# Spreading the filler products of a chunked delta-rule stage one by one, with the chunks written out

## Chip, cores and metric

One NeuronCore of one Trainium2 chip. The metric is the device time of the whole kernel in microseconds (us), the median over executions on the chip. Lower is better.

## The reference, cut to what matters

One decoder block over 2048 tokens of width 1024: a mixer (four gated delta-rule heads beside a gated short convolution, one input and one output projection), a cross-attention into 256 memory tokens, and a SwiGLU feed-forward part. The change lies in the mixer:

```
A = where(strict, einsum(k_beta, k) * decay, 0)
T = triangular_solve(eye + A, eye)          # per chunk and head
u, w = T @ (v * beta), T @ (k_beta * exp(gc))
def step(state, ...):                        # one chunk after the other
    v_new = u_n - w_n @ state
    o     = qd_n @ state + a_n @ v_new
    state = state * exp(gl_n) + kd_n^T @ v_new
...
y = sc_b * causal_depthwise_conv(sc_c * sc_h, conv_sc_w)   # short convolution
```

The chip kernel works in tiles of 128 tokens, which it also calls chunks. The precision is that of fp32: a wide product is three TensorE passes over a high and a low half of each operand.

## The kernel before

The tokens are done in two halves of 1024. In each half come the projection of q, k, v and z, then **the chunk stage** (8 chunks of 128 tokens, four heads at once), then the output projection, attention and the feed-forward part. Every engine runs its own hand-ordered program, and semaphores tie them together.

**The steps of a chunk** are named in `STEPS`: `gram` (transposes of k and the products k·k and q·k, PE lines 1842 and 1845, and transposes of v, line 1858), `a1t` (transposes of the first level's masked matrix, line 1865), then the inverse of the triangular matrix by six doubling levels `y1 x1 ... y6 x6`. In `y` PE multiplies the odd columns of X by a masked block of A (line 1875) and transposes the even columns (line 1887). ScalarE (ACT) copies both results to SBUF (Ym line 1014, Tm line 1018). In `x` PE multiplies Tm and Ym (line 1897), and VectorE (DVE) subtracts the result from X (line 1522) and copies the next even columns (Xe, line 1429). Then come `w` (k times the state, line 1908), `v` (X times the right-hand side, line 1917) and `o` (output and state update, lines 1924, 1928, 1933). DVE makes the right-hand side for `v` in line 1532. GpSimd (POOL) makes the masked blocks `am` for the levels (line 716), the low halves of squares and weights (lines 682 and 2352), and masks the decays (lines 691 to 697).

**The fillers.** The short steps wait for each other, so PE does the short convolution's projections between them: per pair of chunks three weight units (slots 0, 1, 2), two column halves and eight k tiles, each k tile being one *slice* of three 128x512 products (lines 3018, 3019, 3020). `FILL` says how many slices follow each step. A chunk has 24 slices, which are 72 products. A filler waits for its weights' low half (`w_lo_ready`) and, where a unit begins, for the copy or product of its bank on ACT or DVE.

**The order around them.** A pair of chunks (`par` 1, then `par` 0 of the next pair) is the body of a hardware loop of three rounds. Chunk 0 and chunk 7 stand outside it. PE sums the short convolution's squares in line 1825, the norms' squares in lines 1808 and 1810, and transposes the outputs of the chunk before in line 1817.

Of the kernel before, what the change touches and what calls it, by code (L numbers as in the profile page):

```python
# [10 lines left out]
P = 128  # L11
# [161 lines left out]
CHUNK_SLICES = 3 * NCH * KT // 2  # L173
assert sum(FILL) == sum(FILL_FIRST) == CHUNK_SLICES

def block_kernel(nc, x, mem, w_units, w_ab, conv_w, sc_w, a_log, dt_bias, gdn_g, sc_g,
                 g_mix, g_mem, g_x, g_ffn, g_fin, out):
    ctx = ExitStack()
    with ctx:  # L180
# [519 lines left out]
        def chunk_pool(pool, half, m, par, j, last, split_lo):  # L700
# [20 lines left out]
            for step in STEPS:  # L721
                if step == "gram":
                    blocks(1)
                    blocks(2)
                if step in ("y1", "y2", "y3", "y4"):
                    blocks(int(step[1]) + 2)
                if step == "y4":
                    if not last:
                        squares_lo(pool, n + 1, sq_hi)
                    split_lo((n_u + 2, 2, 2) if par == 0 else (n_u + 4, 1, 1), 4)  # L730
                if step == "y6" and par == 0:
                    split_lo((n_u + 3, 0, 0), 4)
                if step == "x6" and not last:
                    decays_pool(pool, n + 1, m + 1, 1 - par)
# [202 lines left out]
        def ln_norms(act, n, b=6):  # L937
# [42 lines left out]
        def start_act(act, half):  # L980
            n = half * TT
            ln_norms(act, n, 5)
# [5 lines left out]
        def chunk_act(act, half, m, par, j, first, last, split_hi):  # L988
# [3 lines left out]
            R = half * 4 + j  # L992
            for step in STEPS:
# [15 lines left out]
                if step[0] == "y":  # L1009
                    act.wait_ge(S["y_full"], n * 6 + l)  # L1010
                    act.wait_ge(S["xy_full"], n * 6 + l - 1)
# [6 lines left out]
                    act.activation(hflat(Tm[:, :, :]), bank(2 if l == 1 else 5)[:, 0:2 * P],  # L1018
# [3 lines left out]
                if par == 0 and step == "y2":  # L1022

                    act.wait_ge(S["sc_full0"], R * 3 + 1)
                    act.wait_ge(S["sc_halo_out"], R)
                    act.activation(sc_u[:, 2:2 + CH], bank(0), ACT.Copy).then_inc(S["c_out"], 1)
                if par == 0 and step == "y6":
                    act.wait_ge(S["sc_full1"], R * 3 + 1)
                    act.activation(sc_u[:, 2 + CH:2 + 2 * CH], bank(1), ACT.Copy)\
                        .then_inc(S["c_out"], 1)  # L1030
                if par == 0 and step == "y6":
                    split_hi(nth_load(half, L_MIX + j + 1, 0), 0, 0)
                if par == 0 and not first:
# [4 lines left out]
                    if step == "y4":  # L1038
                        sc_rms(act, R - 1, 1)
# [9 lines left out]
                if step == ("y4" if first else "x3"):  # L1049
# [6 lines left out]
                if step == "y4":  # L1056
                    if not first:
                        store_o(act, half, m - 1)
                    if not last:
                        load_z(act, half, m + 1, 1 - par)  # L1060
                if step == "y5" and not last:
# [332 lines left out]
        def output_scale(dve, n):  # L1394

            k = n * 4
# [4 lines left out]
            dve.tensor_tensor(ost["v"][:, :], ost["u"][:, :], ost["t"][:, :], ALU.mult)\  # L1401
                .then_inc(S["ostep"], 1)
            dve.wait_ge(S["ostep"], k + 2)
            dve.tensor_scalar(ost["w"][:, :], ost["v"][:, :], -0.5, 1.5, ALU.mult, ALU.add)\
                .then_inc(S["ostep"], 1)
            dve.wait_ge(S["ostep"], k + 3)
            dve.tensor_tensor(ost["r"][:, :], ost["w"][:, :], ost["y"][:, :], ALU.mult)\
                .then_inc(S["ostep"], 1)

        def outputs_scaled(dve, n):  # L1410

            dve.wait_ge(S["ostep"], n * 4 + 4)
# [12 lines left out]
        def even_columns(dve, n, l):  # L1425

            dve.wait_ge(S["x_ready"], n * LEVELS + l)
            dve.wait_ge(S["xt_full"], n * 6 + l - 1)
# [50 lines left out]
        def chunk_dve(dve, half, m, par, j, first, last):  # L1479
# [7 lines left out]
            for step in STEPS:  # L1487
                l = int(step[1]) if step[0] in "yx" else 0
                if step == "gram":

                    if not first:
                        output_scale(dve, n - 1)
                    dve.wait_ge(S["gram_full"], n + 1)
                    dve.wait_ge(S["decm_ready"], n * 3 + 3)
                    dve.tensor_tensor(two(am0[:, :, :]), gram[:, :, :, 0, :], two(am0[:, :, :]),
                                      ALU.mult).then_inc(S["am0_ready"], 1)
                    dve.tensor_tensor(two(A[:, 0, :, :]), gram[:, :, :, 0, :], two(A[:, 0, :, :]),
                                      ALU.mult).then_inc(S["a_ready"], 1)
                if step == "a1t":
# [8 lines left out]
                    even_columns(dve, n, 1)  # L1508
                    if not first:
                        outputs_scaled(dve, n - 1)  # L1510
                    if par == 1:
                        sc_u_product(dve, R, 0)
                    elif not first:
                        sc_y_product(dve, R - 1, 1)
                if step == "y1":
                    dve.tensor_tensor(two(A[:, 1, :, :]), gram[:, :, :, 1, :], two(A[:, 1, :, :]),
                                      ALU.mult).then_inc(S["attn_ready"], 1)
                if step[0] == "x":

                    dve.wait_ge(S["xy_full"], n * 6 + l)  # L1520
                    dve.wait_ge(S["x_ready"], n * LEVELS + l)
                    dve.tensor_tensor(
                        odd_blocks(Xm[:, :, :], l), odd_blocks(Xm[:, :, :], l),
                        bank(4)[:, 0:NH * P // 2].rearrange("p (m c) -> p m c", c=1 << l),
                        ALU.subtract).then_inc(S["x_ready"], 1)
                    if l < LEVELS - 1:
                        even_columns(dve, n, l + 1)
                if step == "x6":
# [7 lines left out]
                    last_rest.then_inc(S["vrest_ready"], 1)  # L1536
                if step == "x1":
# [266 lines left out]
        def sums_norm(pe, n, hi=sq_hi, b=6):  # L1804
# [23 lines left out]
        def chunk_step_pe(pe, half, m, par, j, step, first, last):  # L1828
# [6 lines left out]
            if step == "gram":  # L1835

                pe.wait_ge(S["kqn_ready"], n * 2 + 2)
                pe.wait_ge(S["vrest_ready"], n)
                if first:
                    pe.wait_ge(S["egb_ready"], n + 1)  # L1840
                for hh in range(NH):
# [8 lines left out]
                pe.wait_ge(S["s_ready"], n * 4)  # L1850
                if first:
# [8 lines left out]
            if step == "a1t":  # L1860
                pe.wait_ge(S["am0_ready"], n + 1)

                pe.wait_ge(S["scln_ready"], R * 2 if par == 1 or first else R * 2 - 1)
# [3 lines left out]
            if step[0] == "y":  # L1867
                pe.wait_ge(S["x_ready"], n * LEVELS + l)
                pe.wait_ge(S["am_ready"], n * 6 + l)
                if l == 1:  # L1870
                    pe.wait_ge(S["vb_ready"], n + 1)
                else:
                    pe.wait_ge(S["ym_ready"], n * 12 + 2 * (l - 1))
# [6 lines left out]

                pe.wait_ge(S["xe_ready"], n * 6 + l)
                if l == 2:
                    pe.wait_ge(S["attn_ready"], n + 1)
                elif l > 2:
                    pe.wait_ge(S["t_ready"], n * 6 + l - 1)
                for q in range(2):
                    t = nc.tensor.transpose(bank(2 if l == 1 else 5)[:, q * P:(q + 1) * P],
                                            Xe[:, q, :], ident[:, :])
                t.then_inc(S["xt_full"], 1)
            if step[0] == "x":  # L1890

                pe.wait_ge(S["ym_ready"], n * 12 + 2 * l)
                pe.wait_ge(S["t_ready"], n * 6 + l)
                if l == 1:
                    pe.wait_ge(S["on_ready"], n)
# [4 lines left out]
            if step == "w":  # L1900

                pe.wait_ge(S["s_ready"], n * 4)
                if last:
                    pe.wait_ge(S["oo_ready"], n)
                else:
                    pe.wait_ge(S["rln_ready"], n + 2)
# [33 lines left out]
            if step == "x5" and not last:  # L1940
                if first:
                    pe.wait_ge(S["kdec_ready"], n + 1)
                else:
                    pe.wait_ge(S["oo_ready"], n)
                sums_norm(pe, n + 1)
            if step == "y3" and par == 0 and not first:
                sc_sums(pe, R - 1, 1)
            if step == "o" and par == 1 and not last:
                sc_sums(pe, R, 0)
# [320 lines left out]
        def _(pool):  # L2270
# [75 lines left out]
            def split_lo(n, pieces=1):  # L2346
# [3 lines left out]
                for i in range(pieces):  # L2350
# [3 lines left out]
                last.then_inc(S["w_lo_ready"], 1)  # L2354
# [15 lines left out]
            for half in range(NHALF):  # L2370
# [7 lines left out]
                chunk_pool(pool, half, 0, 0, 0, False, split_lo)  # L2378
                with pool.Fori(0, 3) as j:
                    chunk_pool(pool, half, j * 2 + 1, 1, j, False, split_lo)  # L2380
                    chunk_pool(pool, half, j * 2 + 2, 0, j + 1, False, split_lo)
                chunk_pool(pool, half, TT - 1, 1, 3, True, split_lo)
# [59 lines left out]
        def _(act):  # L2442
# [191 lines left out]
            for half in range(NHALF):  # L2634
# [57 lines left out]
                chunk_act(act, half, 0, 0, 0, True, False, split_hi)  # L2692
                with act.Fori(0, 3) as j:
                    chunk_act(act, half, j * 2 + 1, 1, j, False, False, split_hi)
                    chunk_act(act, half, j * 2 + 2, 0, j + 1, False, False, split_hi)
                chunk_act(act, half, TT - 1, 1, 3, False, True, split_hi)
# [80 lines left out]
        def _(dve):  # L2777
# [96 lines left out]
            for half in range(NHALF):  # L2874
# [18 lines left out]
                chunk_dve(dve, half, 0, 0, 0, True, False)  # L2893
                with dve.Fori(0, 3) as j:
                    chunk_dve(dve, half, j * 2 + 1, 1, j, False, False)
                    chunk_dve(dve, half, j * 2 + 2, 0, j + 1, False, False)
                chunk_dve(dve, half, TT - 1, 1, 3, False, True)
# [117 lines left out]
        def _(pe):  # L3015
# [291 lines left out]
            for half in range(NHALF):  # L3307
# [27 lines left out]
                def qkvz_pe(j, final):  # L3335
                    R = half * NH + j
                    for u in range(4):
                        n = unit(half, U_QKVZ + j * 4 + u)
                        pe.wait_ge(S["w_lo_ready"], n + 1)
                        for c in range(NCH):  # L3340
# [11 lines left out]
                            for k in range(KT):  # L3352
                                if final and g == 7 and k == KT // 2:
                                    gc_broadcast()
                                if final and g == 7 and k == KT - 1:
                                    sums_norm(pe, half * TT, sq_first, 5)
# [12 lines left out]
                def chunk_pe(m, par, j, first, last):  # L3369
# [3 lines left out]
                    done = par * CHUNK_SLICES  # L3373
                    for step, fill in zip(STEPS, FILL_FIRST if first else FILL_LAST if last else FILL):
                        chunk_step_pe(pe, half, m, par, j, step, first, last)
                        for s in range(done, done + fill):
                            u, c, k = s // (NCH * KT), s // KT % NCH, s % KT
# [143 lines left out]
```

## Time and profile before

| | us |
|---|---|
| median of 3 runs (2923.04 to 2924.25) | 2923.35 |
| span of the profiled execution, first to last instruction | 2921.6 |
| PE busy, of the span | 2881.8 (99%) |
| chunk stage of the first half, 316.65 to 588.49 | 271.84 |
| chunk stage of the second half, 1713.93 to 1986.10 | 272.17 |

The profiled execution's own time was not recorded apart from its span. The median of the runs is 1.75 us above the span, for what lies around the first and the last instruction. How to read the profile: PE is TensorE's matmuls and PEld its weight loads, which overlap them. The ends of matmuls are modelled and overlap the next start, so distances are read from start to start. An instruction that stands next to its predecessor has no idle note, and where there is one it is in brackets with its releaser. "issue" is idle time in which the engine waited for nothing that the profile shows.

### The profile page before, as it was taken

Reading aid. Unit: us, or ns where it says so; the run is one execution under the profiler, and the core shown is the slowest. Engines: PE = TensorE matmul, PEld = TensorE weight load, DVE = VectorE, ACT = ScalarE, POOL = GpSimd, SP = SyncE. Lnnn points to the kernel's source line nnn. Section 1 sums busy time; section 2 is a strip of 40 time slices with the busy share of each in tenths; the row PEclk is TensorE's granted clock in tenths of the full one; section 3 lists DMA queues with packets and bytes.
Section 4 is the critical chain, followed back from the end, with each engine's and each line's share of the span. In section 5 each row is a group of like instructions: output and inputs, shape, how many; then the busy total and the mean of one; then the engine's idle time right before and its main releaser. Section 6 shows DMA issues by size and latency. Waiting matters only on the chain.

```text
span 2921.6 us, 43014 instructions
## 1 busy us (share of the span) xinstructions
PE 2881.8 (99%) x14070; PEld 2394.2 (82%) x14070; DVE 1859.1 (64%) x2636; ACT 1145.3 (39%) x2049; POOL 1479.3 (51%) x1214
## 2 busy tenths in 40 slices
PE   8999999999999999999999999999999999999998
PEld 8888788888888888887888878888888888888786
DVE  2565566655359777777877556665634866665778
ACT  5532545434234333334543254443423433333334
POOL 7422455452226555568972244445322655555886
PEclk9999999999999999999999999999999999999999
DMA  7522222151113444467643232224111222224764
GB/s 260 209 96 102 94 80 72 61 177 51 58 72 114 165 152 163 165 222 246 228 144 144 100 109 73 72 65 166 65 44 74 82 108 108 97 93 146 260 192 169
DMA packets 179210, 372.41 MB, mean 127 GB/s; under 512 B 17104, under 2 KB 58128, under 8 KB 179088
## 3 DMA queue, kind: packets, MB, share of 16 engines
q1 hardware_dynamic: 116592, 301.06, 29.6%
q10 hardware_dynamic: 62496, 69.78, 7.0%
q8 instruction: 70, 1.15, 0.2%
q14 instruction: 52, 0.43, 0.0%
HBM read 268.51 MB, written 102.27 MB: 127 GB/s over the span
## 4 chain that ended last, share of the span: by engine, by line
PE 93%; DVE 2%; DMA 1%; POOL 1%; issue 1%; ACT 1%; SPq 0%; DVEq 0%; ACTq 0%; POOLq 0%
PE PS L3018 21%; PE PS L3020 21%; PE PS L3019 21%; PE PS L1991 2%; PE PS L1995 2%; PE PS L1993 2%; PE PS L1964 2%; PE PS L1962 2%; PE PS L1963 2%; PE PS L1875 2%; PE PS L3056 2%; PE PS L3052 2%; PE PS L3054 2%; PE PS L1897 2%; PE PS L3034 1%
## 5 line engine op out<-in xcount | busy, mean ns | idle before, releaser
L3018 PE MATMUL PS<-act_hi,w_hi 128*128 128x512 f32 (+1 forms) x1080 | 424.9, 393 | 1.0 <-POOL w_lo L2327 0.7
L774 POOL TENSOR_TENSOR down_lo<-down_raw,down_hi 128x1024 fp32r<-128x1024 f32 (+1 forms) x196 | 390.8, 2029 | 49.5 <-ACT down_hi L1248 49.2
L3020 PE MATMUL PS<-act_hi,w_lo 128*128 128x512 f32 (+1 forms) x1080 | 403.1, 373 | 0.0
L3019 PE MATMUL PS<-act_lo,w_hi 128*128 128x512 f32 (+1 forms) x1080 | 402.0, 372 | 0.0
L2352 POOL TENSOR_TENSOR w_lo<-raw,w_hi 128x256 fp32r<-128x256 f32 (+1 forms) x144 | 209.4, 1477 | 357.0 <-ACT w_hi L2447 357.0
L740 POOL TENSOR_TENSOR part_lo<-sum_s,part_hi 128x512 fp32r<-128x512 f32 x176 | 235.3, 1344 | 226.8 <-ACT part_hi L1228 226.3
L1705 DVE TENSOR_TENSOR copied<-copied,PS 128x512 f32<-128x512 f32 x264 | 177.4, 686 | 230.9 <-PE PS L3020 221.6
L3018 PE MATMUL PS<-op_t_hi,part_hi 128*128 128x512 f32 x704 | 274.4, 390 | 0.3 <-issue 0.2
L3020 PE MATMUL PS<-op_t_hi,part_lo 128*128 128x512 f32 x704 | 273.9, 389 | 0.0
L3019 PE MATMUL PS<-op_t_lo,part_hi 128*128 128x512 f32 x704 | 273.9, 389 | 0.0
L1789 DVE TENSOR_TENSOR h<-h,PS 128x512 f32<-128x512 f32 x344 | 218.1, 678 | 62.3 <-PE PS L3020 43.6
L1248 ACT ACTIVATE down_hi<-down_raw 128x1024 fp32r<-128x1024 f32 x154 | 159.4, 1057 | 240.4 <-PE PS L3020 131.4
L3018 PE MATMUL PS<-down_hi 128*128 128x512 f32 x616 | 241.9, 393 | 6.8 <-DVE h L1789 6.4
L3020 PE MATMUL PS<-down_hi,down_lo 128*128 128x512 f32 x616 | 240.3, 390 | 0.0
L3019 PE MATMUL PS<-down_lo,down_hi 128*128 128x512 f32 x616 | 240.2, 390 | 0.0
L3020 PEld LDWEIGHTS PS<-act_hi,w_lo 128*128 128x128 f32 x1080 | 203.5, 188 | 36.4
L3018 PEld LDWEIGHTS PS<-act_hi,w_hi 128*128 128x128 f32 x1080 | 204.2, 189 | 30.3 <-issue 2.6
L3019 PEld LDWEIGHTS PS<-act_lo,w_hi 128*128 128x128 f32 x1080 | 204.5, 189 | 28.5 <-issue 1.9
L3018 PE MATMUL PS<-op_b_hi,part_hi 128*128 128x512 f32 x528 | 205.9, 390 | 0.0
L3020 PE MATMUL PS<-op_b_hi,part_lo 128*128 128x512 f32 x528 | 205.4, 389 | 0.0
L3019 PE MATMUL PS<-op_b_lo,part_hi 128*128 128x512 f32 x528 | 205.4, 389 | 0.0
L1228 ACT ACTIVATE part_hi<-sum_s 128x512 fp32r<-128x512 f32 x176 | 109.2, 629 | 221.2 <-PE PS L3020 159.8
(368 smaller groups left out, 6432.1 us busy)
## 6 DMA issues: line engine op xcount, KB each, us to landing
raw<-in_w_units SPq DMA_DIRECT2D x132, 512.0 KB, 3.9
a_d<-copied SPq DMA_DIRECT2D x154, 256.0 KB, 2.2
down_raw<-a_d SPq DMA_DIRECT2D x154, 256.0 KB, 3.6
gu_raw<-in_w_units SPq DMA_DIRECT2D x44, 512.0 KB, 4.7
down_raw<-t_d SPq DMA_DIRECT2D x88, 256.0 KB, 3.0
down_raw<-in_w_units SPq DMA_DIRECT2D x66, 256.0 KB, 3.0
qkvz_d<-stage ACTq DMA_DIRECT2D x64, 256.0 KB, 2.5
raw<-att_d SPq DMA_DIRECT2D x32, 512.0 KB, 3.2
```

The lines of the kernel that those rows point to most:

```text
L740: pool.tensor_tensor(lo[:, :], part_source(s, k), hi[:, :].bitcast(f32), ALU.subtract)\
L774: last = pool.tensor_tensor(flat(lo[:, :, :])[:, cs], flat(down_raw[m % 4][:, :, :])[:, cs], flat(hi[:, :, :])[:, cs].bitcast(f32), ALU.su ...
L1228: act.activation(part[k][0][:, :], part_source(s, k), ACT.Copy)\
L1248: act.activation(flat(down_part[m][0][:, :, :]), flat(down_raw[m % 4][:, :, :]), ACT.Copy)\
L1705: dve.tensor_tensor(buf[dst][:, :], buf[a][:, :], bank(k), ALU.add)\
L1789: dve.tensor_tensor(dst, dst, b, ALU.subtract if s % 7 == 6 else ALU.add)\
L1875: t = nc.tensor.matmul(bank(3)[:, q * P:(q + 1) * P].rearrange("p (m c) -> p m c", c=1 << l), am[:, l % 2, 2 * q:2 * q + 2, :].rearrange(" ...
L1897: t = nc.tensor.matmul(bank(4)[:, q * P:(q + 1) * P], Tm[:, q, :], Ym[:, q, :], start=True, stop=True)
L2352: last = pool.tensor_tensor(w_lo[slot][:, cs], raw[raw_slot][:, cs], w_hi[slot][:, cs].bitcast(f32), ALU.subtract)
L3018: nc.tensor.matmul(out_ap, whi, xhi, start=start, stop=False)
L3019: nc.tensor.matmul(out_ap, whi, xlo, start=False, stop=False)
L3020: return nc.tensor.matmul(out_ap, wlo, xhi, start=False, stop=stop)
```

## The change

- The filler is counted in single products instead of slices of three, in new lists by chunk kind. A regular chunk still has 72; the first has 84 and the second 60. PE has a new step `vt` (the transposes of v) apart from `gram`, with fillers between them, and its `w` now stands ahead of `x6`.
- All eight chunks are written out on PE, ACT, DVE and POOL; there is no hardware loop left in the stage.
- POOL makes the low half of the next weight unit in pieces at `y1`, `y2` and `y3`, where it had stood at `y4` or `y6`. ACT makes the matching high half at `y1`, and its copies of bank 1 and the high half of slot 0 leave `y6`.
- DVE multiplies the first level's matrix as soon as the second of POOL's three decay steps is done. It forms X and Xe ahead of the output scale, which has three operations instead of four, and puts the `attn` product in `y2` and the right-hand side for `v` (line 1532) ahead of the last subtraction from X.
- PE's transposes of the even columns use bank 2 at every level, and the norms' sums use banks 5 and 6. Some waits move to another step or change places.

The diff, cut to its core:

```diff
-FILL = [0, 0, 2, 2] + [2, 1] * 6 + [2, 0, 0]
-FILL_LAST = [0, 0, 2, 2] + [2, 1] * 6 + [2, 0, 0]
-FILL_FIRST = [0, 6, 0, 2] + [1, 1] * 6 + [2, 1, 1]
+PE_STEPS = ["start", "gram", "vt", "a1t"] + [f"{x}{l}" for l in range(1, LEVELS - 1) for x in "yx"] + \
+    ["y6", "w", "x6", "v", "o"]
+FILL = [0, 2, 3, 7] + [6, 5, 6, 5, 5, 5, 6, 5, 6, 1] + [1, 3, 5, 1, 0]
+FILL_FIRST = [14, 2, 2, 9] + [6, 4, 6, 4, 6, 4, 6, 4, 6, 2] + [0, 3, 5, 1, 0]
+FILL_SECOND = [0, 2, 2, 6] + [6, 4, 6, 4, 5, 4, 5, 4, 6, 0] + [0, 2, 4, 0, 0]
+FILL_LAST = [0, 2, 3, 7] + [6, 5, 6, 5, 5, 5, 6, 5, 6, 5] + [0, 2, 4, 0, 0]
...
+                if step in ("y1", "y2", "y3") and m > 0:
+                    early = (n_u + 3, 0, 0) if par else (n_u + 2, 2, 2)
+                    split_lo(early, 4, range(2, 4) if step == "y3" else [int(step[1]) - 1])
...
-                if par == 0 and step == "y6":
-                    act.wait_ge(S["sc_full1"], R * 3 + 1)
-                    act.activation(sc_u[:, 2 + CH:2 + 2 * CH], bank(1), ACT.Copy)\
-                        .then_inc(S["c_out"], 1)
-                if par == 0 and step == "y6":
+                if first and step == "y4":
+                    copy_c(1)
+                if par == 1 and step == "y1":
                     split_hi(nth_load(half, L_MIX + j + 1, 0), 0, 0)
...
-                    if not first:
-                        output_scale(dve, n - 1)
+                    dve.wait_ge(S["decm_ready"], n * 3 + 2)
                     dve.wait_ge(S["gram_full"], n + 1)
-                    dve.wait_ge(S["decm_ready"], n * 3 + 3)
                     dve.tensor_tensor(two(am0[:, :, :]), gram[:, :, :, 0, :], two(am0[:, :, :]),
...
-                pe.wait_ge(S["s_ready"], n * 4)
+            if step == "vt":
...
+                pe.wait_ge(S["s_ready"], n * 4)
                 for hh in range(NH):
                     t = nc.tensor.transpose(r4(bank(3))[:, hh, :], vv[:, par, hh, :], ident[:, :])
...
-                pe.wait_ge(S["x_ready"], n * LEVELS + l)
-                pe.wait_ge(S["am_ready"], n * 6 + l)
                 if l == 1:
                     pe.wait_ge(S["vb_ready"], n + 1)
-                else:
-                    pe.wait_ge(S["ym_ready"], n * 12 + 2 * (l - 1))
+                    pe.wait_ge(S["am_ready"], n * 6 + l)
+                pe.wait_ge(S["x_ready"], n * LEVELS + l)
...
             if step[0] == "x":
+                if l == 1:
+                    pe.wait_ge(S["on_ready"], n)
+                if l < LEVELS - 1:
+                    pe.wait_ge(S["am_ready"], n * 6 + l + 1)
...
-                chunk_pe(0, 0, 0, True, False)
-                with pe.Fori(0, 3) as j:
-                    chunk_pe(j * 2 + 1, 1, j, False, False)
-                    chunk_pe(j * 2 + 2, 0, j + 1, False, False)
-                chunk_pe(TT - 1, 1, 3, False, True)
+                for m in range(TT):
+                    chunk_pe(m, m % 2, m // 2, m == 0, m == TT - 1)
```

## Rows read from the trace of the kernel before

**Rows 1.** Page, section 1: busy time, share and instructions of each engine.

```profile
PE 2881.8 (99%) x14070; PEld 2394.2 (82%) x14070; DVE 1859.1 (64%) x2636; ACT 1145.3 (39%) x2049; POOL 1479.3 (51%) x1214
```

**Rows 2.** Windows: chunk stages, chunks 0, 1, 6, 7; length, busy (instructions), clock.

```profile
316.65:588.49 271.84, 269.79 (x1587) 222.53 (x1587) 174.33 (x345) 131.38 (x273) 131.51 (x149) 1.00 0.25 78
1713.93:1986.10 272.17, 269.96 (x1587) 222.63 (x1588) 174.33 (x345) 131.44 (x273) 131.61 (x149) 1.00 0.25 78
316.65:348.33 31.68, 30.06 (x179) 23.92 (x179) 16.97 (x32) 17.55 (x34) 17.87 (x21) 1.00 0.37 123
348.33:382.75 34.42, 34.39 (x204) 28.60 (x202) 23.93 (x47) 15.12 (x32) 16.93 (x19) 1.00 0.21 64
521.49:556.16 34.67, 34.61 (x203) 28.56 (x202) 20.91 (x44) 19.33 (x39) 16.18 (x20) 1.00 0.24 76
556.16:588.49 32.33, 32.30 (x199) 27.28 (x197) 20.54 (x45) 10.44 (x26) 12.18 (x15) 1.00 0.19 57
```

**Rows 3.** PE's timeline, chunk 6 (in the loop): start, length, line.

```profile
527.54 0.62 PE L1875 MATMUL PS<-Xm,am 128*128 128x128 f32 x4
...
528.13 0.48 PE L3018 MATMUL PS<-act_hi,w_hi 128*128 128x512 f32 x1
...
529.60 0.61 PE L1897 MATMUL PS<-Ym,Tm 128*128 128x128 f32 x4
529.96 0.48 PE L3018 MATMUL PS<-act_hi,w_hi 128*128 128x512 f32 x1
...
530.90 0.68 PE L1875 MATMUL PS<-Xm,am 128*128 128x128 f32 x4
...
531.56 0.47 PE L3018 MATMUL PS<-act_hi,w_hi 128*128 128x512 f32 x1
...
533.03 0.60 PE L1897 MATMUL PS<-Ym,Tm 128*128 128x128 f32 x4
...
550.00 1.05 PE L1908 MATMUL PS<-state,kqn 128*128 128x128 f32 x8
550.81 0.48 PE L3018 MATMUL PS<-act_hi,w_hi 128*128 128x512 f32 x1
...
552.46 1.13 PE L1917 MATMUL PS<-vb,Xm 128*128 128x128 f32 x8
```

**Rows 4.** PE's timeline, chunk 7 and chunk 0 (both outside the loop).

```profile
574.79 0.61 PE L1897 MATMUL PS<-Ym,Tm 128*128 128x128 f32 x4
...
575.93 0.70 PE L1875 MATMUL PS<-Xm,am 128*128 128x128 f32 x4
...
316.65 0.66 PE L1842 MATMUL PS<-ident,kqn 128*128 128x128 f32 x4 [0.83 <-DVE kqn L1381]
...
324.78 0.68 PE L1875 MATMUL PS<-Xm,am 128*128 128x128 f32 x4
...
326.62 0.68 PE L1897 MATMUL PS<-Ym,Tm 128*128 128x128 f32 x4 [0.24 <-ACT Tm L1018]
```

**Rows 5.** Waits of PE's weight loads, first half's stage: total, times, longest.

```profile
PEld PS L1875 <- issue: 9.9, 24, 0.4
...
PEld PS L1858 <- DVE state L1587: 2.5, 6, 0.4
```

**Rows 6.** Timelines of DVE and POOL, chunk 6.

```profile
530.25 0.42 DVE L1522 TENSOR_TENSOR Xm<-Xm,PS 128x256 f32<-128x256 f32 x1 [1.00 <-PE PS L1897]
530.70 0.29 DVE L1429 COPY Xe<-Xm 128x256 f32<-128x256 f32 x1
...
545.83 0.76 DVE L1429 COPY Xe<-Xm 128x256 f32<-128x256 f32 x1
...
551.18 1.13 DVE L1532 SCALAR_TENSOR_TENSOR vb<-PS,gate_nbeg,vb 128x128 f32<-128x128 f32 x4 [1.26 <-PE PS L1908]
...
543.41 3.77 POOL L2352 TENSOR_TENSOR w_lo<-raw,w_hi 128x256 fp32r<-128x256 f32 x4
```

**Rows 7.** DMA queue of instructions, 316 to 590 us: packets, MB, share.

```profile
q8 instruction: 7, 0.11, 0.2%
```

More of the change, by code:

```diff
@@ L729, in chunk_pool @@
                         squares_lo(pool, n + 1, sq_hi)
-                    split_lo((n_u + 2, 2, 2) if par == 0 else (n_u + 4, 1, 1), 4)
-                if step == "y6" and par == 0:
-                    split_lo((n_u + 3, 0, 0), 4)
+                    if m == 0:
+                        split_lo((n_u + 2, 2, 2), 4)
+                    if par == 1:
+                        split_lo((n_u + 4, 1, 1), 4)
                 if step == "x6" and not last:
@@ L981, in start_act @@
             n = half * TT
-            ln_norms(act, n, 5)
+            ln_norms(act, n)
             exp_decays(act, n, 0)
@@ L992, in chunk_act, with copy_c @@
             R = half * 4 + j
+            def copy_c(c):
+                act.wait_ge(S[f"sc_full{c}"], R * 3 + 1)
+                act.activation(sc_u[:, 2 + c * CH:2 + (c + 1) * CH], bank(c), ACT.Copy)\
+                    .then_inc(S["c_out"], 1)
             for step in STEPS:
@@ L1048, in chunk_act @@
                     squares(act, half, m + 1, 1 - par)
-                if step == ("y4" if first else "x3"):
+                if step == ("y4" if first or par == 1 else "y1"):
                     act.wait_ge(S["sc_full1"], R * 3 + 2 * par)
@@ L1060, in chunk_act @@
                         load_z(act, half, m + 1, 1 - par)
+                    if par == 0 and not first:
+                        copy_c(1)
                 if step == "y5" and not last:
@@ L1902, in chunk_step_pe @@
                 pe.wait_ge(S["s_ready"], n * 4)
[L1903 to L1906, printed above, removed]
+                pe.wait_ge(S["kdec_ready"], n + 1)
+                pe.wait_ge(S["oo_ready"], n)
                 for hh in range(NH):
@@ L2344, in _, with split_lo @@
                 .then_inc(made(), 1)
-            def split_lo(n, pieces=1):
+            def split_lo(n, pieces=1, which=None):
                 number, slot, raw_slot = n
                 pool.wait_ge(S["w_hi_ready"], number + 1)
-                for i in range(pieces):
+                for i in range(pieces) if which is None else which:
                     cs = slice(i * D // pieces, (i + 1) * D // pieces)
@@ L2353, in split_lo @@
                                               w_hi[slot][:, cs].bitcast(f32), ALU.subtract)
-                last.then_inc(S["w_lo_ready"], 1)
+                if i == pieces - 1:
+                    last.then_inc(S["w_lo_ready"], 1)
             def att_lo(half, i):
@@ L2377, in _ @@
                 decays_pool(pool, half * TT, 0, 0)
[L2378 to L2382, printed above, removed]
+                for m in range(TT):
+                    chunk_pool(pool, half, m, m % 2, m // 2, m == TT - 1, split_lo)
                 for c in range(4):
@@ L2691, in _ @@
                 load_z(act, half, 0, 0)
[L2692 to L2696, printed above, removed]
+                for m in range(TT):
+                    chunk_act(act, half, m, m % 2, m // 2, m == 0, m == TT - 1, split_hi)
                 end_act(act, half)
@@ L2892, in _ @@
                 start_dve(dve, half)
[L2893 to L2897, printed above, removed]
+                for m in range(TT):
+                    chunk_dve(dve, half, m, m % 2, m // 2, m == 0, m == TT - 1)
                 def first_add(t):
@@ L3355, in qkvz_pe @@
                                 if final and g == 7 and k == KT - 1:
-                                    sums_norm(pe, half * TT, sq_first, 5)
+                                    sums_norm(pe, half * TT, sq_first)
                                 last = col_slice(PS[:, b, :], u, c, k)
@@ L3372, in chunk_pe @@
                     n_u = unit(half, U_MIX + j * 3)
-                    done = par * CHUNK_SLICES
-                    for step, fill in zip(STEPS, FILL_FIRST if first else FILL_LAST if last else FILL):
+                    done = sum(FILLS[m - 1]) if par else 0
+                    for step, fill in zip(PE_STEPS, FILLS[m]):
                         chunk_step_pe(pe, half, m, par, j, step, first, last)
                         for s in range(done, done + fill):
-                            u, c, k = s // (NCH * KT), s // KT % NCH, s % KT
-                            if k == 0:
+                            u, c, k, i = s // (3 * NCH * KT), s // (3 * KT) % NCH, s // 3 % KT, s % 3
+                            if k == 0 and i == 0:
                                 if c == 0:
@@ L3387, in chunk_pe @@
                                     pe.wait_ge(S["u_ready"], R * 2 + c + 1)
-                            product = col_slice(PS[:, c, :], u, c, k)
-                            if k == KT - 1:
+                            ks, cs = slice(k * P, (k + 1) * P), slice(c * CH, (c + 1) * CH)
+                            product = nc.tensor.matmul(
+                                PS[:, c, :], (w_lo if i == 2 else w_hi)[u][:, ks],
+                                (act_lo if i == 1 else act_hi)[:, k, cs],
+                                start=k == 0 and i == 0, stop=k == KT - 1 and i == 2)
+                            if k == KT - 1 and i == 2:
                                 product.then_inc(S[f"sc_full{c}"], 1)
                         done += fill
-                chunk_pe(0, 0, 0, True, False)
-                with pe.Fori(0, 3) as j:
-                    chunk_pe(j * 2 + 1, 1, j, False, False)
-                    chunk_pe(j * 2 + 2, 0, j + 1, False, False)
-                chunk_pe(TT - 1, 1, 3, False, True)
+                for m in range(TT):
+                    chunk_pe(m, m % 2, m // 2, m == 0, m == TT - 1)
                 n = half * TT + TT - 1
```

84 lines of the change are left out of this document (40 added, 44 removed).

## The prediction

> **What bounds the kernel now.** I read busy times first. PE is busy for 2881.8 of 2921.6 us, no other engine for more than 64% [rows 1], so PE alone sets the end. Two gains are possible: less work on PE, or less waiting inside what counts as busy, because modelled matmul ends hide short gaps. The change removes no PE instruction: a pair of chunks keeps 144 filler products and all its small matmuls. So it can only remove waits, and only in the two chunk stages, 271.84 and 272.17 us, run at full granted clock [rows 2]. Next come the windows of single chunks: 31.68 us for chunk 0, 34.42 for chunk 1, 34.67 for chunk 6 in the loop, 32.33 for chunk 7 [rows 2]. The last view is the distance from start to start on PE, compared between a chunk in the loop and one outside.
>
> **Prices that everything uses.** Six fillers take 1.47 us (531.56 to 533.03) [rows 3]. An `x` step takes 0.36 up to its first filler (529.60 to 529.96) [rows 3]. In chunk 7 it takes 1.14 in all (574.79 to 575.93) [rows 4], so three fillers take 0.78. A further product costs (1.47 - 0.78) / 3 = 0.23, and the first of a run 0.32. An unstalled `y` takes 0.59 to its first filler (527.54 to 528.13), one that had to wait 0.66 (530.90 to 531.56) [rows 3]: a stop costs 0.07 more than its gap, since weight loads no longer run ahead.
>
> **Waits in a loop chunk (34.67).**
> - `x` to the next `y`: 1.30 (529.60 to 530.90) [rows 3] against 1.14 in chunk 7 [rows 4], although the work and the three fillers are the same. That is 0.16, at four levels in each of six loop chunks; the view of waits counts 24 on line 1875, called "issue" [rows 5]. Four times (0.16 + 0.07) is 0.92.
> - ahead of `v`: 550.81 to 552.46 is 1.65 against 1.47 [rows 3], with the restart 0.25.
> - ahead of the transposes of v: the state update is late in all chunks but 0 and 1 [rows 5]. Chunk 1 lacks it and is 34.67 - 34.42 = 0.25 shorter [rows 2].
> - Sum 1.42. A few restarts of 0.06 elsewhere I leave out.
>
> **Waits outside the loop.** Chunk 7 has the 0.25 ahead of line 1858, five restarts of 0.07, and about 0.15 at `v`: 0.75. Without them it would take 31.6. Chunk 0 has 54 fillers after its first matmul instead of 72, four products for the norms that chunk 7 lacks, and none of the four transposes of outputs (about 0.4, as the row of line 1842 lasts 0.66 with its tail [rows 4]). Unstalled it would take 31.6 - 18 x 0.23 + 4 x 0.23 - 0.4 = 28.0; it takes 31.68, so 3.7 us are waits. The pattern agrees: with three fillers `y` to `x` is 1.84 (324.78 to 326.62), and PE waits for the copy Tm [rows 4].
>
> **What the change does to each wait.**
> - Level chains: the shortest possible `y` to `x` is about 1.84 [rows 4], `x` to `y` at most 1.14 without the loop [rows 4]. The new `y` has six fillers, 0.59 + 1.47 = 2.06, or five, 1.83. The new `x` has five, 0.36 + 0.32 + 4 x 0.23 = 1.60, or four, 1.37. All clear their chain but the five-filler `y`, which is on the edge: one or two a chunk, 0.07 each. Even if the 0.16 is a longer chain (1.30) and no cost of the loop, 1.37 covers it.
> - `vt` with two products ahead adds 0.55 where 0.25 was missing: gone.
> - `w` ahead of `x6`: line 1908 starts at 550.00 and its eight matmuls take 0.81 [rows 3]; DVE begins line 1532 at 551.18, 1.18 after, and needs 1.13 [rows 6], so it is done 2.31 after `w` begins. `x6` starts 0.81 + 0.32 + 2 x 0.23 = 1.59 after `w`. Its product reaches DVE 0.65 after its start (529.60 [rows 3], 530.25 [rows 6]), at 2.24, so the subtraction now waits for line 1532 and starts at 2.31 instead. It needs 0.42 and 0.23 to the next PE start (530.67 to 530.90) [rows 3, 6]: 2.96. The natural start of `v` is 1.59 + 1.60 = 3.19. The swap is hidden by 0.2 us. Should DVE come late to line 1532 by more than that, `v` waits, and `o`, the kqn of the next chunk and its `gram` with it.
> - ACT's copy and high half leave `y6`, where they stood between norms and decays. At `y1`, `y2`, `y4` they follow the Tm copy. ACT is busy for 19.33 of 34.67 us in chunk 6 and POOL for 16.18 [rows 2], and a level lasts 2.06 + 1.60 = 3.66. POOL's quarter (3.77 / 4 = 0.94 [rows 6]) stands behind ACT's high half and ahead of the block that `x3` needs, two levels or 7 us on. The weight load on SP's queue is released by low halves that are now made earlier. I take nothing for this; if the cover is gone, POOL's blocks stop `x3`.
> - DVE's shorter output scale, X first, `attn` in `y2`: the old order didn't stop `y1`, so nothing.
> - Chunk 0 starts when kqn is ready (316.65, after 0.83 idle [rows 4]); fewer products before it only lengthen the idle. The first pair thus has 130 fillers after this point instead of 126: 4 x 0.23 = 0.93 lost.
>
> **Sum for a half.** Chunks 2 to 6: 5 x 1.42 = 7.1. Chunk 1: 1.17. Chunk 7: 0.75. Chunk 0: 3.7 - 0.93 = 2.8. Together 11.8. Against it stand eight five-filler `y` (0.6). From both sides: no new stop gives 11.8 or, with the small restarts, 12.6; if each new edge (`y3`, `v`, one Xe copy beside POOL) costs 0.25 a chunk, 8 x 0.6 = 5 goes. I take 11.4, as most edges clear. Two halves: 22.8. The stages follow one another on PE, and what comes after waits for PE, so it stays: span 2921.6 - 22.8 = 2898.8, and 1.75 more outside the span as in the runs: **2900.5 us**.
>
> **Rivals.**
> - *The code in a straight line stops PE.* In the first stage four bodies of chunk code (chunk 0, two in the loop, chunk 7) drew 7 packets of instructions [rows 7]. Written out there are eight, so some 7 more packets a half, 14 in all. To eat the gain each must stop PE for 22.8 / 14 = 1.6 us; from 2.05 us each the kernel is more than 0.2% slower, at 2.3 us it takes 2900.5 + 32 = 2933. Against it: chunk 7 is written out already, and PE is busy for 32.30 of its 32.33 us; the whole stage lacks 2.05 us of PE's busy time, 1.6 of which lie in chunk 0 [rows 2]. 3 in 100. By that rule the unrolling has a price; by the rows of chunk 7 it has none.
> - *POOL and the ports.* POOL's quarters now run beside the levels. The Xe copy, 0.29 alone, took 0.76 beside POOL's split [rows 6], and line 1887 waits for it. If 0.25 of that shows at two levels in each of 14 chunks, 7.0 us go: 2907.5. Against: that slow copy was at `y6`, and its chunk took no longer than the others of the loop. 15 in 100.
> - *Only the loop's cost goes.* If the fillers' moves gain what they lose, 24 x 0.23 = 5.5 a half remain: 2912. 7 in 100.
> - *Given back after the stage,* by the loads of the residual or mixer rows that PE's projection waits for. They are released by the last chunk itself, so they shift along. At most all 22.8 go: 2921 to 2923, same. 4 in 100.
> - *More than forecast,* the restarts of 0.06 and those at five fillers too: 2 x 12.6 = 25.2, or a little more, 2896 to 2898. 11 in 100.
>
> **How the numbers follow.** The forecast, 2898 to 2904, has 60 in 100. The range takes in the ports, with two edges more than counted, and the end without any new stop; the loop-only case, same, slower and a few in 100 below 2895 stay outside, which is under 2 in 10: 2895 to 2911. Faster by over 0.2% (5.8 us, what a measurement of this kernel can tell from no change) are the forecast, ports, loop-only and more: 0.93; same 0.04; slower 0.03.
>
> **What would show it.** Loop chunks of 33.2 to 33.4 us from one start of line 1842 to the next (chunks 2 to 6), chunks 0 and 1 together 62 instead of 66.1. PEld's "issue" waits on the `y` product, 9.9 us in the first half [rows 5], near zero, likewise its waits for Ym in chunk 0 and for the state. `x` to `y` 1.6 with five fillers, without a gap. `v` starting right behind the fifth filler of `x6`. The start of chunk 0 unchanged, with some 1.8 us idle before it. The prediction is wrong if PE shows gaps at `v` or at the five-filler `y` above 0.1, gaps that no semaphore explains, or if chunks shrink and the projection behind them starts with a wait.

## The result, and the profile after

The changed kernel takes 2900.35 us (median of 4, 2897.82 to 2903.12) against 2923.19 (4, 2922.93 to 2924.25): a ratio of 0.9922, 95% interval 0.9908 to 0.9936, or 22.8 us. That is faster by more than 0.2%, and within 0.2 us of the forecast; the runs themselves reach over 5 us, so a meeting this close is partly luck. The profiled execution has a span of 2899.6 us and took 2901.37. A second measurement beside other kernels gave 2900.56 (5, 2897.38 to 2901.9), ratio 0.9923, interval 0.9910 to 0.9937. One of the 9 runs of the kernel before that stand beside experiments 5 to 8 took 4841.1 us at a granted clock of 0.556 and is left out of their ratios.

The page's busy times after, to set beside [rows 1]:

```profile
PE 2862.3 (99%) x14070; PEld 2405.0 (83%) x14070; DVE 1851.6 (64%) x2620; ACT 1146.5 (40%) x2049; POOL 1468.4 (51%) x1214
```

PE issues the same 14070 matmuls and is busy 19.5 us less: what went were short gaps that the modelled ends of matmuls had hidden. DVE lost 16 instructions, one of the output scale in each chunk. Windows after, in the order of [rows 2] (two stages, chunks 0, 1, 6, 7):

```profile
317.28:578.03 260.75, 260.06 (x1590) 227.16 (x1591) 169.04 (x338) 131.83 (x273) 125.84 (x149) 1.00 0.27 82
1703.53:1964.30 260.77, 260.08 (x1591) 227.12 (x1591) 169.20 (x338) 131.84 (x273) 125.86 (x149) 1.00 0.27 82
317.28:348.59 31.31, 31.31 (x195) 27.84 (x196) 15.53 (x31) 16.66 (x33) 14.42 (x18) 1.00 0.35 110
348.59:380.32 31.73, 31.30 (x192) 26.53 (x191) 25.32 (x47) 16.06 (x33) 19.24 (x22) 1.00 0.28 84
513.51:546.73 33.22, 33.22 (x204) 28.96 (x203) 19.38 (x43) 18.57 (x38) 13.39 (x18) 1.00 0.26 80
546.73:578.04 31.31, 31.31 (x199) 27.82 (x197) 19.61 (x44) 11.28 (x27) 13.44 (x18) 1.00 0.19 60
```

The stages lose 271.84 - 260.75 = 11.09 and 272.17 - 260.77 = 11.40, together 22.5 of the span's 22.0. The clock was granted in full before and after. What lies between and behind the stages kept its length within 0.3 us, so nothing was given back there; the first stage starts 0.63 us later. PE's timeline in chunk 6, to set beside [rows 3]:

```profile
519.48 0.62 PE L1887 MATMUL PS<-Xm,am 128*128 128x128 f32 x4
...
521.54 0.61 PE L1909 MATMUL PS<-Ym,Tm 128*128 128x128 f32 x4
...
523.14 0.61 PE L1887 MATMUL PS<-Xm,am 128*128 128x128 f32 x4
...
539.73 1.05 PE L1918 MATMUL PS<-state,kqn 128*128 128x128 f32 x8
...
541.32 0.61 PE L1909 MATMUL PS<-Ym,Tm 128*128 128x128 f32 x4
...
542.92 1.06 PE L1927 MATMUL PS<-vb,Xm 128*128 128x128 f32 x8
```

`y` to `x` is 2.06, `x` to `y` 1.60, `w` to `x6` 1.59 and `x6` to `v` 1.60, each what its instructions need. Waits of PE's weight loads in the first stage, beside [rows 5], then the start of chunk 0 beside [rows 4]:

```profile
PEld PS L1856 <- issue: 3.8, 7, 2.2
PEld PS L3389 <- issue: 1.4, 6, 0.2
PEld PS L1873 <- DVE state L1601: 1.4, 3, 0.7
PEld PS L1927 <- issue: 0.8, 2, 0.6
PEld PS L1909 <- DVE osq L1424: 0.6, 1, 0.6
```

```profile
317.28 0.63 PE L1856 MATMUL PS<-ident,kqn 128*128 128x128 f32 x4 [1.80 <-DVE kqn L1395]
```

The 9.9 us on the `y` product are gone. What is left lies at the ends: 1.80 us idle ahead of chunk 0, in chunk 1 the scaled outputs (osq) and `v`, and in chunk 2 the late state.

### The profile page after: what moved, and what is told of

It reads as the page before. It is cut to its first block, busy times and chain, and to the rows that moved or that the text cites. A ratio compares the mean times of both kernels' runs of the same rounds, so it can differ in the third digit from the quotient of the medians.

```text
span 2899.6 us, 41618 instructions
## 1 busy us (share of the span) xinstructions
PE 2862.3 (99%) x14070; PEld 2405.0 (83%) x14070; DVE 1851.6 (64%) x2620; ACT 1146.5 (40%) x2049; POOL 1468.4 (51%) x1214
## 4 chain that ended last, share of the span: by engine, by line
PE 93%; DVE 3%; DMA 1%; POOL 1%; issue 1%; ACT 1%; SPq 0%; DVEq 0%; ACTq 0%; POOLq 0%
PE PS L3018 19%; PE PS L3020 18%; PE PS L3019 18%; PE PS L3389 9%; PE PS L1999 2%; PE PS L2003 2%; PE PS L2001 2%; PE PS L1972 2%; PE PS L1970 2%; PE PS L1971 2%; PE PS L3052 2%; PE PS L3056 2%; PE PS L3054 2%; PE PS L1909 1%; PE PS L1887 1%; PE PS L3034 1%
## 5 line engine op out<-in xcount | busy, mean ns | idle before, releaser
L2360 POOL TENSOR_TENSOR w_lo<-raw,w_hi 128x256 fp32r<-128x256 f32 (+1 forms) x144 | 197.4, 1385 | 348.1 <-ACT w_hi L2453 348.1
L3018 PE MATMUL PS<-act_hi,w_hi 128*128 128x512 f32 (+1 forms) x696 | 253.6, 364 | 0.7 <-POOL w_lo L2335 0.4
L3019 PE MATMUL PS<-act_lo,w_hi 128*128 128x512 f32 (+1 forms) x696 | 251.8, 362 | 0.0
L3020 PE MATMUL PS<-act_hi,w_lo 128*128 128x512 f32 (+1 forms) x696 | 251.8, 362 | 0.0
L2827 DVE TENSOR_TENSOR h<-h,PS 128x1024 f32<-128x1024 f32 x96 | 117.1, 1221 | 120.0 <-PE PS L3056 72.7
L3389 PE MATMUL PS<-act_hi,w_lo 128*128 128x512 f32 x384 | 160.9, 419 | 0.0
L3389 PE MATMUL PS<-act_hi,w_hi 128*128 128x512 f32 x384 | 160.5, 418 | 0.0
```

What stands on the lines that cost most here:

```text
L2360: last = pool.tensor_tensor(w_lo[slot][:, cs], raw[raw_slot][:, cs], w_hi[slot][:, cs].bitcast(f32), ALU.subtract)
L2827: dve.tensor_tensor(h[:, t, :], h[:, t, :], flat(bank(b + 2 * (t % 2), 2)), ALU.add)\
L3018: nc.tensor.matmul(out_ap, whi, xhi, start=start, stop=False)
L3019: nc.tensor.matmul(out_ap, whi, xlo, start=False, stop=False)
L3020: return nc.tensor.matmul(out_ap, wlo, xhi, start=False, stop=stop)
L3389: product = nc.tensor.matmul(PS[:, c, :], (w_lo if i == 2 else w_hi)[u][:, ks], (act_lo if i == 1 else act_hi)[:, k, cs], start=k == 0 and ...
```

## The experiments

All ran beside the kernel before on one chip in each group. I use the first stage's length (start of chunk 0 to the end of chunk 7, one profiled execution) for mechanisms, and medians for verdicts. Before it is 271.84, after 260.75.

**1. Before, chunks written out on all engines.**

```diff
...
-                chunk_pe(0, 0, 0, True, False)
-                with pe.Fori(0, 3) as j:
...
+                for m in range(TT):
+                    chunk_pe(m, m % 2, m // 2, m == 0, m == TT - 1)
```

> The kernel before with its eight chunks written out on PE, DVE, ACT and POOL, nothing else changed. Theory A (the loop itself costs time on PE ahead of the product of line 1875 and ahead of v): the distance from x to y falls from 1.30 to 1.14 us in chunks 1 to 6, a loop chunk from 34.67 to about 33.9, and the kernel to about 2913 (24 times 0.16 and 6 times 0.09 a half). Theory B (1.30 is the chain PE, DVE, PE and has nothing to do with the loop): the distance stays 1.30, time 2923.

2916.57 us (10 runs), ratio 0.9975, interval 0.9966 to 0.9985. In the timeline `x` to the next `y` falls from 1.30 to 1.13:

```profile
527.25 0.61 PE L1897 MATMUL PS<-Ym,Tm 128*128 128x128 f32 x4
...
528.38 0.70 PE L1875 MATMUL PS<-Xm,am 128*128 128x128 f32 x4
```

Chunk 6 takes 34.10 (33.9 expected): a wait for kdec, which the loop's cost had hidden, shows in its place (`y3` to `x3` is 3.66 instead of 3.49). So the loop costs 0.16 where PE stops, and removing it alone brings 6.6 us. The kernel was expected at about 2913; it stayed between the two theories.

**2. The same on PE alone.**

> As e1, but only PE's program is written out; DVE, ACT and POOL keep their loops. If the cost of the loop is PE's own (register arithmetic ahead of its waits): 2913, as e1. If it is DVE or another engine that comes late in its loop: 2923 as before, and x to y stays at 1.30.

2920.25 us (10 runs), ratio 0.9990, interval 0.9980 to 0.9999. `x` to `y` is 1.14 here too, so the 0.16 lies in PE's own loop. The total was expected at 2913 as well. Part of the difference to experiment 1 lies at `v`: from `w` to `v` it is 2.45 here, as before, and 2.36 in experiment 1, in each of chunks 1 to 6. Why is not shown.

**3. The change, with fillers only in threes.**

```diff
-FILL = [0, 2, 3, 7] + [6, 5, 6, 5, 5, 5, 6, 5, 6, 1] + [1, 3, 5, 1, 0]
+FILL = [0, 3, 6, 6] + [6, 3, 6, 3, 6, 3, 6, 3, 6, 3] + [0, 3, 6, 3, 0]
...
```

> The changed kernel with its fillers in runs of three or six only: y 6, x 3 (chunk 1 partly y 3), vt 6, a1t 6, v 3; the order of steps stays. Theory A (single products only save the restart at x to y): x to y 1.14 with 0.07 restarts at four or five levels of 14 chunks, about 5 us above the changed kernel, 2905. Theory B (the exact spread is what carries the gain): 2911 or more.

2913.68 us (5 runs), ratio 0.9965, interval 0.9951 to 0.9979, as theory B had it (2911 or more); stage 266.99. Three fillers behind `x` don't cover the subtraction's chain. The waits of the weight loads:

```profile
PEld PS L1887 <- DVE Xm L1545: 10.6, 33, 0.3
```

**4. The change, with chunks 3 to 6 in a loop of two rounds on every engine.**

> The changed kernel with chunks 3 to 6 back in a hardware loop of two rounds on all four engines. Theory A (the loop costs 0.16 a level only where PE is stopped just before y; five fillers cover it): within 1 us of the changed kernel, 2900, x to y 1.60. Theory B (the loop's cost lies on PE's own queue, whatever stands before the wait): 8 chunks times 5 levels times 0.16 is 6 us, 2906 or more.

2900.69 us (4 runs), ratio 0.9925, interval 0.9908 to 0.9941. The loop costs nothing that can be told once five fillers stand behind `x`: `x` to `y` is 1.60. The gain doesn't come from the straight code. Chunks 0, 1, 2 and 7 stay outside the loop here; a loop over more of them was not tried.

**5. The change, splits of the weights where they were.**

```diff
-                if step in ("y1", "y2", "y3") and m > 0:
...
-                    if m == 0:
+                    if par == 0:
                         split_lo((n_u + 2, 2, 2), 4)
...
+                if step == "y6" and par == 0:
+                    split_lo((n_u + 3, 0, 0), 4)
...
```

> The changed kernel with the halves of the weights split where they were before: ACT's high half of unit 3 in y6 of an even chunk, POOL's low halves in one piece of four at y4 and at y6 of an even chunk. All else, the fillers too, as changed. Theory A (PE alone sets the time; POOL beside DVE's port costs nothing in either place): 2900.5, 2898 to 2904, chunks of 33.2. Theory B (the quarters spread over the levels were needed so that POOL's blocks are in time for the faster levels): PE waits at x3 to x5 or at y6, 0.3 to 1.5 us in every chunk, 2905 to 2920. Theory C (the spread quarters slow DVE's copies at two levels a chunk): this kernel is faster than the changed one by up to 7 us, 2894 to 2898.

2902.15 us (4 runs), ratio 0.9925, interval 0.9909 to 0.9941; stage 261.55. Chunk 5 takes 33.22, as after, so neither place costs in an ordinary chunk. Of the 0.8 us more in the stage 0.7 lie in chunks 0 and 1 (31.52 and 32.22). The medians' 1.8 us are within the runs' spread.

**6. The change, `w` behind `x6` again,** and DVE's line 1536 behind the subtraction.

```diff
-    ["y6", "w", "x6", "v", "o"]
+    ["y6", "x6", "w", "v", "o"]
...
-FILL = [0, 2, 3, 7] + [6, 5, 6, 5, 5, 5, 6, 5, 6, 1] + [1, 3, 5, 1, 0]
+FILL = [0, 2, 3, 7] + [6, 5, 6, 5, 5, 5, 6, 5, 6, 0] + [5, 0, 6, 0, 0]
...
```

> The changed kernel with the exchange of w and x6 undone, on PE and on DVE (subtraction first, then line 1536), fillers of that place dealt out anew: y6 5, x6 0, w 6, their sum as changed. Theory A (the exchange costs nothing, it only lets v be reached with fewer fillers; now v waits for line 1536, about 2.31 after the start of w plus 0.23, against 0.81 + 0.32 + 5 x 0.23 = 2.28 of work): 0.25 to 0.35 a chunk with the restart, 16 chunks, 2904 to 2907. Theory B (the exchange changes nothing either way): 2900.5. Theory C (the exchange itself costs time by DVE's later subtraction): below 2898.

2909.99 us (4 runs), ratio 0.9950, interval 0.9934 to 0.9965; stage 265.40, 4.65 more, twice what theory A gave. Chunks 3 and 5 take 0.9 more than after, chunk 1 1.2, chunk 7 1.0, and chunks 4 and 6 0.2 to 0.3. In chunks 3 and 5 two more things are late. The missing filler behind `x5` lets `y6` wait for Xe, and `x6` comes 0.3 later, a price of my deal. And DVE, which comes later to the right-hand side for `v` (line 1546 of this kernel), ends the next chunk's kqn later: in chunk 3 at 448.78, and its `gram` starts at 448.92, 0.45 more behind the step ahead of it than in the changed kernel. It is the chain that the prediction feared the exchange would make late, and it is late here, in the kernel without the exchange. So the exchange is worth at most about 9 us, my deal's price included; that it gains because `w` and the fillers then cover two chains at once is my reading.

**7 and 8. More fillers ahead of chunk 0.** 8, whose diff this is, moves six from the first pair to its start; 7 does so too, deals 80 and 64 to the pair, and puts sc_u's product behind the output scale in chunk 1.

```diff
-FILL_FIRST = [14, 2, 2, 9] + [6, 4, 6, 4, 6, 4, 6, 4, 6, 2] + [0, 3, 5, 1, 0]
+FILL_FIRST = [20, 2, 2, 6] + [6, 4, 6, 4, 6, 4, 6, 4, 6, 0] + [0, 2, 5, 1, 0]
```

> The changed kernel with six more fillers ahead of chunk 0 (20 instead of 14) and so six fewer behind its start, 80 and 64 fillers in the first pair instead of 84 and 60, and in chunk 1 DVE's product sc_u behind the output scale again. Theory A (the 1.80 us that PE idles ahead of chunk 0 are free, and chunk 1 waits at x1 for the scaled outputs alone): 6 x 0.23 = 1.4 and 0.4 to 0.5 a half less, 2896 to 2897. Theory B (the fillers taken out of the first pair cover chains as tight as elsewhere, so each comes back as a wait): 2900 to 2902.

> The changed kernel with six more fillers ahead of chunk 0 alone (20, then 2, 2, 6 and 0 behind x5, 2 behind w), chunk 1 as changed. Theory A: 1.4 a half less, 2897.5. Theory B: no change, 2900 to 2902.

7: 2895.86 us (5 runs), ratio 0.9904, interval 0.9890 to 0.9918. 8: 2896.53 us (4 runs), ratio 0.9906, interval 0.9890 to 0.9922. Chunks 0 and 1 fall from 31.31 + 31.73 to 29.24 + 31.96 in 7 and 29.98 + 31.73 in 8.

**9. The changed kernel again.**

> The changed kernel itself, once more, beside the three kernels that run with it. 2900.4 as before, 2898 to 2903.

2900.56 us, given above.

**10. The change, fillers dealt wrongly:** same number, same order of all steps.

```diff
-FILL = [0, 2, 3, 7] + [6, 5, 6, 5, 5, 5, 6, 5, 6, 1] + [1, 3, 5, 1, 0]
+FILL = [0, 2, 3, 7] + [4, 7, 4, 7, 4, 7, 4, 7, 4, 2] + [1, 3, 5, 1, 0]
...
```

> The changed kernel with the same products dealt wrongly: four behind each y product and seven (six in the first pair) behind each x product, sums as changed. Theory A (what the change gains is that each run just covers its chain; from y to x no less than about 1.84 are possible, four fillers make 0.59 + 0.32 + 3 x 0.23 = 1.60, so each of five levels waits 0.24 and restarts for 0.07, and the longer x gives nothing): 16 x 5 x 0.31 = 24.8 more, 2925, as slow as before the change, with chunks of 34.8. Theory B (the order and the straight code gain, and the deal of the fillers matters little): 2900 to 2906.

2920.62 us (10 runs), ratio 0.9991 to before, interval 0.9982 to 1.0001: 20.1 us more than the changed kernel, nearly all of its gain. Stage 270.84. I had counted five levels; at `y3` the transposes of outputs stand beside the fillers, and it doesn't stop. 16 x 4 x 0.31 = 19.8 is close to what was measured. The view of waits names POOL's next block at 17 of the 32 stops, as the changed kernel waits for it at `x` too; but in the timeline of chunk 6 that block ends at 526.47, ACT's Tm at 526.73 and `x` starts 0.15 behind it, so it is the copies that PE waits for:

```profile
525.74 0.73 POOL L720 TENSOR_TENSOR am<-dec,even_mask 128x256 f32<-128x256 f32 x1 [1.29 <-PE PS L1887]
526.35 0.38 ACT L1033 ACTIVATE Tm<-PS 128x256 f32<-128x256 f32 x1
526.88 0.68 PE L1909 MATMUL PS<-Ym,Tm 128*128 128x128 f32 x4
```

**11. Before, with single fillers as the only edit:** loop, order, waits and splits kept.

```diff
-FILL = [0, 0, 2, 2] + [2, 1] * 6 + [2, 0, 0]
+FILL = [0, 0, 5, 7] + [6, 5, 6, 5, 5, 5, 6, 5, 6, 0] + [5, 0, 6, 0, 0]
...
```

> The kernel before with its loop, its order of steps, waits and splits, and only the fillers as single products: y 6 or 5, x 5, w 6, x6 none, 18 ahead of chunk 0, 72 in each chunk. Theory A (the fillers carry the change, and five behind x cover the loop's 0.16): loop chunks lose 4 x 0.23 and chunks 0 and 7 about 1 and 0.4, they keep the 0.25 ahead of the transposes of v and some of that at v: 6.5 to 8 a half, 2907 to 2910. Theory B (the reordering is needed for the fillers to pay): 2916 or more.

2921.77 us (10 runs), ratio 0.9993, interval 0.9984 to 1.0002: no change. My theory A fell here. In the stage of 271.13 chunks 1 to 7 have next to no wait inside the first five levels any more (`y` to `x` 2.05, `x` to `y` 1.60), and all the time saved there came back at the ends of chunks; chunk 0 gained 1.29 and chunk 7 lost 0.49. Waits of the weight loads:

```profile
PEld PS L1858 <- DVE state L1587: 4.7, 7, 0.8
PEld PS L1917 <- issue: 4.3, 8, 1.0
...
PEld PS L1897 <- ACT Ym L1014: 3.1, 5, 0.6
PEld PS L1908 <- issue: 2.1, 7, 0.4
```

Timeline of chunk 6 and the start of chunk 7, lines of PE, ACT, DVE and POOL:

```profile
547.03 1.14 ACT L929 ACTIVATE dec<-diff 128x512 f32<-128x512 f32 x2
...
548.65 0.38 ACT L1018 ACTIVATE Tm<-PS 128x256 f32<-128x256 f32 x1
548.93 1.02 ACT L941 ACTIVATE rn<-PS 128x1024 f32<-128x1024 f32 x1
...
549.18 0.68 PE L1897 MATMUL PS<-Ym,Tm 128*128 128x128 f32 x4 [0.24 <-ACT Tm L1018]
...
550.09 1.13 PE L1908 MATMUL PS<-state,kqn 128*128 128x128 f32 x8 [0.23 <-ACT rn L941]
```

```profile
556.99 0.99 DVE L1581 TENSOR_SCALAR ost_t<-ost_ss 128x4 f32<-128x4 f32 x1
...
559.06 0.66 PE L1858 MATMUL PS<-ident,vv 128*128 128x128 f32 x4 [0.40 <-DVE state L1587]
```

```profile
551.46 3.71 POOL L2352 TENSOR_TENSOR w_lo<-raw,w_hi 128x256 fp32r<-128x256 f32 x4 [3.62 <-ACT w_hi L2447]
555.12 1.49 POOL L691 TENSOR_TENSOR dec<-dec,gate_beta 128x512 f32<-128x512 f32 x1
```

`x6` waits for ACT, which works off the next chunk's decays first; `w` then waits for ACT's norms (the wait on rln_ready that the change replaces), 0.91 behind `x6` (0.61 in the odd chunks) where an `x` needs 0.36; `v` for line 1532; and the transposes of v stand right behind `gram` with the state 0.4 late, as a DVE step on 128x4 elements took 0.99 (0.62 in the kernel before, 0.30 after). POOL works on the decays' masks at that time in all three, so its work alone doesn't explain the difference; the cause is open.

This is one deal. It puts no filler between `x6` and `w`, where the kernel before has three. Whether another deal in the old order gains something was not tried, so the experiment shows that single fillers are not enough by themselves, not that they gain nothing in any deal.

**12. As 7, with 21 fillers at the start and 5 behind a1t.**

> As e7_start_and_second, with one filler more ahead of chunk 0 and one less behind its a1t. Theory A (PE still idles 0.47 ahead of chunk 0 and a1t has slack): 0.2 a half less than e7, 2895.4, and 4 to 5 us less than the changed kernel of the same job. Theory B (the gain seen in e7 was spread between jobs): within 2 us of the changed kernel.

2895.52 us (4 runs), ratio 0.9908 to before, interval 0.9892 to 0.9923; 5.0 less than the changed kernel of the same group, whose runs reach from 2897.38 to 2901.9. The stage takes 259.02, and PE idles for 0.28 ahead of chunk 0:

```profile
314.82 0.63 PE L1853 MATMUL PS<-ident,kqn 128*128 128x128 f32 x4 [0.28 <-DVE kqn L1395]
```

This is the best version, about 27 us below before. It can't be told from 7.

## Why the prediction was right, point by point

- **PE sets the time, and only waits inside the two chunk stages can go.** Right: the stages hold 22.5 of 22.0 us.
- **Chunks 2 to 6: 7.1 a half.** Measured 173.41 - 166.41 = 7.00. Its parts hold one by one: `x` to `y` 1.60 without a gap, `y` unstalled, `v` right behind the fifth filler. Chunks 3 to 6 take 33.2 as forecast; chunk 2 takes 33.55, as it still waits 0.34 for the state.
- **Chunk 7: 0.75.** Measured 32.33 - 31.31 = 1.02. I had left its small restarts out, which is the likely rest (1.89 instead of 1.83 behind the transposes of v, for one).
- **Chunks 0 and 1: 2.8 + 1.17, ending at 62.** Measured 63.04, 3.06 less than before. This term was over-sized by 0.9: chunk 1 has only 60 fillers and waits for the scaled outputs at `x1` (0.36 and its restart) and at `v` (0.41 and its restart). By the forecast's prices chunk 0 would take 28.0 + 16 x 0.23 = 31.68 and chunk 1 34.42 - 1.17 - 12 x 0.23 = 30.49; they took 31.31 and 31.73. The gap of 0.41 at `v` is also above the 0.1 that the forecast named as a sign of being wrong: true of this one chunk, not of the others. The idle 1.8 us ahead of chunk 0 came as forecast, and experiments 7, 8 and 12 show that they could be had.
- **Edges taken off, 0.4 a half.** The five-filler `y` that I feared at 0.07 is `y3` in most chunks, where the transposes of outputs stand beside the fillers: it costs nothing. In chunk 1 `y4` has five too, and the `y` behind it comes 0.08 later (1.45 instead of 1.37). The feared Xe copy beside POOL costs about 0.1 at `y5` in chunks 3 and 5 (2.14 to 2.16 up to `x5` instead of 2.05). That chunk 1 was over-sized, chunk 7 under-sized and 0.4 taken off for edges nearly cancels, so 11.4 was forecast and 11.09 and 11.40 came. The mechanism was right; the closeness of the total is in part luck.
- **The exchange of `w` and `x6` hidden by 0.2 us.** Right to the step: line 1536 starts 1.09 after `w` (1.18 forecast) and the subtraction 2.30 (2.31). Its rows in the changed kernel:

```profile
540.82 1.13 DVE L1536 SCALAR_TENSOR_TENSOR vb<-PS,gate_nbeg,vb 128x128 f32<-128x128 f32 x4 [1.98 <-PE PS L1918]
...
542.03 0.42 DVE L1545 TENSOR_TENSOR Xm<-Xm,PS 128x256 f32<-128x256 f32 x1
```

- **Edits costed at nothing.** This is the weak step. As costs, nothing was right. But I never priced what happens without them, and left the wait of `w` on the norms out altogether. Experiment 11 shows that single fillers, in its one deal, gain 0.7 us a stage in the old surroundings, where I expected 6.5 to 8: each wait removed inside the levels was met again behind them. Experiment 3 shows the other half: the new surroundings with fillers in threes gain 4.85 of 11.09. The two gains by themselves, 0.7 and 4.85, make half of what both bring together. The exchange of `w` and `x6` is worth up to 4.65 of it; how the rest divides over `vt` with its fillers, ACT's order and the wait of `w` was not separated.
- **Rivals.** Ports: two places for POOL's splits differ by 0.8 us a stage, nearly all in the first pair, so not the 7 us. The slow copy exists in the changed kernel, beside POOL's squares (line 686) and not its quarters, and costs the 0.1 named above, in two chunks:

```profile
434.16 0.79 DVE L1440 COPY Xe<-Xm 128x256 f32<-128x256 f32 x1
432.68 2.86 POOL L686 TENSOR_TENSOR sq_lo<-rn,sq_hi 128x256 fp32r<-128x256 f32 x4
```

- **The other rivals.** Only the loop's cost: its removal alone is worth 6.6 us, and the change brings more than three times that. Straight-line code: the first stage drew 13 packets of instructions where [rows 7] have 7, six more where some seven were forecast, and chunk 6 shows no gap at all (33.22 of 33.22 busy). The Trainium skill (Advanced Engine Details and Errata, ISA Cache) gives the instruction cache's size and its lines; a price of code written out does not follow from that alone, and none is visible here:

```profile
q8 instruction: 13, 0.21, 0.3%
```

## What to carry to other kernels

When short independent products fill an engine's waits, count for each link of the chain the time from start to start that it can't go below, and give it just that many; one product too few at four links cost 20 us here, and the products moved behind the next link gained nothing. Before crediting a removed wait, ask which wait comes next with everything else unchanged: a chunk that gets faster inside meets its neighbours' chains at both ends, and those must be moved in the same edit. A cost of stopping (0.16 in a loop, 0.07 for the restart) vanishes by never stopping; writing the loop out isn't needed for it.

## What the runs showed of the hardware beyond that

- **A DMA issue on ACT can stop PE.** The issue of the load of line 862 (line 854 in the kernel before) usually takes 0.4 to 0.8 us; in 8 of the 14 profiles it took 1.30 to 2.17 once or twice. ACT's copies behind it then come late, and PE waits at one `x` product. That makes single chunks of 33.4 to 34.0 us instead of 33.2 in experiments 4, 8, 9 and 12. In experiments 1 and 2 it was line 849's issue in chunk 0 (0.95 and 0.78 instead of 0.51), with the first `x` 0.44 and 0.49 later. In experiment 8:

```profile
533.02 2.17 ACTq L862 DMA_DIRECT2D zz<-qkvz_d  x1
535.23 0.60 ACT L1005 ACTIVATE sc_u<-PS 128x512 f32<-128x512 f32 x1 [2.00 <-issue]
...
536.84 0.68 PE L1909 MATMUL PS<-Ym,Tm 128*128 128x128 f32 x4 [0.58 <-ACT Tm L1033]
```

- **The stretch ahead of the first chunk varies between executions** (chunk 0 starts at 314.68 in one profile of the changed kernel and at 317.28 in the other), which is 2.6 of the 4.0 us between these two executions. Stage lengths repeat much better: 260.75 and 260.98.
